# Index scores of a sparse attention step: the order of projection halves, cached products, index chunks and convolution taps on one Trainium2 core

## The chip, the cores and the metric

The kernel runs on one core of one Trainium2 chip. The metric is the device time of one execution in microseconds (us). Three runs of the kernel before took 1020.48, 1022.67 and 1022.98 us; their median, 1022.67 us, is the time before.

## The reference, cut to what matters

One step of a hybrid decoder layer for a prompt group of 1024 tokens and a sample group of 8 tokens over a paged cache of 8192 keys each. One input projection (1024 to 4168 columns) feeds sparse attention and a gated convolution branch. An indexer chooses 256 keys for every query, which are then attended:

```python
def _index_select(qi, wi, ki, q_pos, k_pos, k_sel):
    s = jnp.einsum('thd,ld->thl', qi, ki).astype(jnp.float32) * (IDX_DIM ** -0.5)
    score = jnp.einsum('th,thl->tl', wi.astype(jnp.float32) * (N_IDX_HEADS ** -0.5), jax.nn.relu(s))
    score = jnp.where(k_pos[None, :] <= q_pos[:, None], score, -jnp.inf)
    _, idx = lax.top_k(score, k_sel)
    return idx.astype(jnp.int32)
```

The prompt uses it with its own 1024 index keys, the samples with the cached index keys (`cache_k_idx`). The convolution branch is a causal depthwise convolution of width 31 over 512 channels, with LayerNorm and SiLU behind it. Both branches are gated, go through one output projection and are added to the input. Everything is float32.

## The kernel before, in words

**Stages.** Five instruction streams are written out by hand (TensorE = PE, ScalarE = ACT, VectorE = DVE, GpSimd = POOL, SyncE = SP). They meet only at semaphores, and each engine takes its stream in order. The stages are: normalise and transpose x; project the weight groups in the order kw, glub, glua, qi, v, ga, gc, k, q (line 41 on); index scores; a bitwise search for the 256th largest score; selection, with the k and q projections beside it; attention; output projection. Every PE operation goes through `mm` (L529), so most PE rows carry that line; `plan` hands out the eight PSUM banks, and `begin` waits until the former user of a bank has drained it.

**Convolution taps.** `taps` (L1319, instruction at L1340) runs on DVE. There are 4 channel blocks (c) with 31 taps (j) each, 124 in all, block after block. A tap is one multiply-add over 128x1024 into an accumulator `ctmp`, and waits for the tap before it (`taps_done`). Tap 0 of block c waits for POOL's product of the two gates, `u_done`. Between stretches of taps, DVE does the queries' and weights' operands for the cached scores, the own-key score (`snew_ready`, which PE waits for in `own_score` behind tile 0 of v), and `cached_turn(0)` and `cached_turn(1)`.

**Cached index scores, eight groups n.** POOL gathers pages into `cin` (L1852, four transfers per group, each into a buffer that `cached_turn` of the group before has freed). `cached_turn(n)` (L1306) is four DVE transposes into `ct`, each waiting for its transfer and for PE's product of group n-1 to be through with that buffer. `cached(n)` (L684) on PE multiplies them with the queries and then does the weighted sum of group n-1 (`weigh`); after group 7, that of 7 too. `cached_out(n)` (L1101) and `scores_out` on ACT evacuate them into `sc16a` or `sc16b`, and SP writes each pair to DRAM and reads the whole back as `SD`. `sc16b` lies on the part of `SC` that holds query block 7, so the first index sum of block 7 waits for its last transfer (`scd_out[1]`).

**Prompt index scores, 40 chunks.** `CHUNKS` runs over query blocks i = 2..7, head pairs hp = 0..3 and key columns in steps of 512. Blocks 2 and 3 have one chunk for each head pair (384 and 512 columns), blocks 4 to 7 have two: 512 and a rest of 128, 256, 384 or 512. A chunk holds two units, one for each head e: PE fills two banks at the same time with the two row halves of the array (`index_scores`, L702; two pairs of banks, so chunk n waits for chunk n-2 to be drained); ACT takes each unit through a relu into one of four `relu` buffers (`index_relu`, L1114, instruction L1122), once DVE has used the buffer's last content; DVE weighs it and adds it into `SC` (`weighted`, L1379; L1389 for the first head, L1392 for the others). Each sum waits for the sum just before it (`relu_used`), which is the one it adds to or its neighbour.

**The order of this stage.** Nine slots, the same on PE, ACT and DVE (L715, L1142, L1394). A slot holds one tile of v (8 matmuls of 512 columns; `between` is called in its middle), half of the slot's chunks in the middle of the tile, one cached product, the other half of the chunks, and another cached product. Slots 0 to 4 have no chunks; slots 5, 6 and 7 have 10, 11 and 11; slot 8 the last eight (all of block 7). The cached products stand at the end of slots 1 and 4 (groups 0 and 1), and in slots 5, 6, 7 twice each (2 and 3, 4 and 5, 6 and 7).

**The search.** 32 rounds: DVE (L1420) and ACT (L1159) count how many scores reach a candidate, PE sums the sample's counts over a group of partitions (`group_sum`, L559), and DVE makes the next candidate (L1474). Two more counts (rounds 32 and 33) follow. PE's stream has projection units beside it, `STAGE_UNITS`: the last, 8-row tile of v, 12 pieces of ga and 12 of gc (8 matmuls of 344 columns each), and the first `K_EARLY` = 4 tiles of k (8 matmuls of 512). `pace` (L568) puts one of 34 group sums in front of the matmul at which a multiple of `COLUMNS_PER_SUM` = (all columns)/35 is reached: 86528 columns, 2472 per sum. PE then waits there until the count of that round is in. 

**Behind the search.** The loop over `NORMED` (k tiles 0 to 8, then q) has on PE: tile n if n >= `K_EARLY` (L808), at n = 3 `equal_before` (waits for DVE's `equals_counted`), the transposes of tile n-3, `chosen_before`; on DVE: `norm(n)`, with `chosen` behind tile 0, which waits for `equal_before`.

## Time and profile before

| | |
|---|---|
| median of three runs | 1022.67 us |
| the profiled execution, its own time | 1022.88 us |
| span of the profiled execution | 1021.0 us |
| busy PE, DVE, ACT, POOL | 918.9, 690.4, 348.6, 84.4 us |
| mean granted TensorE clock | 0.947 of 2.4 GHz |

The sums of the prediction are differences of the span (first to last instruction). The profiled execution's own time is 1.9 us more than its span, and 0.2 us above the median. A line of the timeline gives the start and the length of a run of like instructions, and in brackets how long the engine stood idle before it and who ended that. A float32 matmul shows as two records, so "x16" is eight matmuls.

### The profile page before, as it was taken

How to read it: one execution, taken by the hardware profiler on the slowest of the kernel's cores; microseconds unless marked ns; L12 is line 12 of the kernel's file. 1: busy time of each engine (PE TensorE's matmuls, PEld its weight loads, DVE VectorE, ACT ScalarE, POOL GpSimd, SP SyncE). 2: the span in 40 equal slices, each digit the busy share in tenths (PEclk: the TensorE clock that was granted, in tenths of full speed). 3: DMA queues.
4: the chain of work that ended last, by engine and by line, in shares of the span. 5: the costliest groups of instructions: out<-in, count | busy, mean ns of one | idle time of the engine just before them, and what ended most of it. 6: DMA issues, size and time to landing. Idle time of an engine off the chain costs nothing.

```text
span 1021.0 us, 11394 instructions
## 1 busy us (share of the span) xinstructions
PE 918.9 (90%) x3952; PEld 508.5 (50%) x3952; DVE 690.4 (68%) x1532; ACT 348.6 (34%) x750; POOL 84.4 (8%) x89
## 2 busy tenths in 40 slices
PE   3999999999988679999969898797697889999998
PEld 2866666664332236666534244453465555445432
DVE  4218999998587788888898888956587564332101
ACT  6311101101344568888600000313855363321000
POOL 0120112001133000000000000001011010310000
PEclk9899999999999979999989799798799799999999
DMA  8272011213255050020030000005021111321111
GB/s 298 92 206 27 1 47 39 84 47 119 83 167 168 16 177 30 1 83 1 0 103 32 11 31 1 1 1 214 21 64 52 32 35 39 124 83 41 64 63 43
DMA packets 35459, 69.90 MB, mean 68 GB/s; under 512 B 9625, under 2 KB 12097, under 8 KB 35393
## 3 DMA queue, kind: packets, MB, share of 16 engines
q1 hardware_dynamic: 28233, 43.99, 13.3%
q0 software_dynamic: 7168, 25.17, 7.6%
q8 instruction: 32, 0.52, 0.2%
q14 instruction: 26, 0.21, 0.1%
HBM read 58.52 MB, written 11.11 MB: 68 GB/s over the span
## 4 chain that ended last, share of the span: by engine, by line
PE 78%; DVE 13%; ACT 3%; issue 3%; DMA 1%; SPq 1%; DVEq 0%; POOL 0%; ACTq 0%; POOLq 0%
PE ps L529 74%; PE ps L532 5%; DVE SC L1392 2%; DVE ct L1314 1%; DMA xn<-in_x_prompt 1%; DVE pv L1570 1%; ACT PTs L1018 1%; DVE eqm L1420 1%; ACT uT L1191 1%; DVE LB L1571 1%; DVE uT L1776 0%; ACT relu L1122 0%; ACT sqj L1031 0%; DVE junk L1420 0%; DVE zN L1594 0%
## 5 line engine op out<-in xcount | busy, mean ns | idle before, releaser
L529 PE MATMUL ps<-xT,W 128*128 128x344 f32 x960 | 286.9, 457 | 0.0
L529 PEld LDWEIGHTS ps<-xT,W 128*128 128x128 f32 x960 | 180.9, 191 | 90.8 <-issue 3.5
L529 PE MATMUL ps<-W,xT 128*128 128x512 f32 (+3 forms) x576 | 224.8, 546 | 0.0
L1340 DVE SCALAR_TENSOR_TENSOR ctmp<-uT,chw,ctmp 128x1024 f32<-128x1024 f32 x116 | 153.0, 1319 | 4.0
L529 PEld LDWEIGHTS ps<-W,xT 128*128 128x128 f32 (+1 forms) x576 | 95.8, 188 | 114.4 <-issue 113.8
L1159 ACT ACTIVATE sgj<-SC,cand,sense 128x1024 bf16<-128x1024 f32 (+2 forms) x96 | 104.4, 1088 | 25.8 <-DVE cand L1474 20.8
L1018 ACT ACTIVATE PTs<-ps 128x512 f32<-128x512 f32 (+3 forms) x96 | 43.0, 483 | 128.2 <-PE ps L532 123.5
L1807 DVE TENSOR_TENSOR ps<-ps,TP 128x256 f32<-128x256 f32 (+1 forms) x64 | 26.4, 412 | 69.4 <-PE ps L529 69.0
L1204 ACT ACTIVATE nsq<-ps 128x512 f32<-128x512 f32 (+1 forms) x18 | 10.7, 596 | 163.2 <-DVE nss L1583 115.8
L532 PE MATMUL ps<-Cc,Pm 128*128 128x128 f32 x288 | 47.3, 304 | 17.6 <-ACT PTs L1018 17.0
L529 PE MATMUL ps<-W,uT 128*128 128x512 f32 x128 | 60.1, 613 | 0.0
L529 PE MATMUL ps<-W,qT 128*128 128x512 f32 x128 | 58.8, 601 | 0.0
L1812 DVE CUSTOM_DVE_ANT_0 Pm<-ps,SC 128x1024 f32<-128x1024 f32 (+7 forms) x64 | 48.5, 758 | 9.9 <-PE ps L532 7.9
L532 PEld LDWEIGHTS ps<-Cc,Pm 128*128 128x128 f32 x288 | 34.6, 154 | 40.8 <-issue 39.0
L1420 DVE TENSOR_SCALAR_CACHE_REDUCE junk<-SC,cand 128x768 bf16<-128x768 f32 (+2 forms) x67 | 54.6, 815 | 0.0
L1787 DVE TENSOR_TENSOR resid<-resid,ps 128x512 f32<-128x512 f32 (+1 forms) x18 | 12.3, 684 | 60.8 <-PE ps L529 60.8
L1218 ACT ACTIVATE Pm<-Pm,mn 128x1024 f32<-128x1024 f32 (+7 forms) x64 | 49.5, 774 | 9.4 <-DVE mn L1812 8.8
L1885 POOL DMA_INDIRECT KVr<-in_cache_k,idx x16 | 16.0, 1000 | 438.3 <-DVE zq L1598 336.9
L529 PE MATMUL ps<-kiT,qiT 64*128 64x512 f32 (+3 forms) x160 | 37.0, 570 | 15.6 <-ACT relu L1122 15.1
L1392 DVE SCALAR_TENSOR_TENSOR SC<-relu,wI,SC 128x512 f32<-128x512 f32 (+3 forms) x70 | 45.9, 656 | 7.6 <-ACT relu L1122 0.8
L1852 POOL DMA_INDIRECT cin<-in_cache_k_idx,pidx x32 | 34.5, 1079 | 179.6 <-DVE ct L1314 141.9
L1122 ACT ACTIVATE relu<-ps 128x512 f32<-128x512 f32 (+3 forms) x80 | 38.5, 524 | 31.4 <-PE ps L529 16.7
(309 smaller groups left out, 1007.6 us busy)
## 6 DMA issues: line engine op xcount, KB each, us to landing
W<-in_w_in SPq DMA_DIRECT2D x8, 2048.0 KB, 8.9
xn<-in_x_prompt SPq DMA_DIRECT2D x8, 512.0 KB, 7.7
W<-in_w_out SPq DMA_DIRECT2D x1, 4096.0 KB, 13.7
resid<-in_x_prompt SPq DMA_DIRECT2D x16, 256.0 KB
out<-resid SPq DMA_DIRECT2D x16, 256.0 KB
out<-V SPq DMA_DIRECT2D x8, 256.0 KB
out<-zN SPq DMA_DIRECT2D x8, 256.0 KB, 2.0
bias_rows<-tprow SPq DMA_DIRECT2D x1, 1536.0 KB
```

The costliest lines, as they stand in the source:

```text
L529: return nc.tensor.matmul(out, lhsT, rhs, start=start, stop=stop)
L532: return nc.tensor.transpose(out, in_, ident[0:n, 0:n])
L1018: nc.scalar.activation(out, in_, func, scale=scale).then_inc(plan.drain_sem(tag), 1)
L1122: nc.scalar.activation(relu[:, u % 4, 0:width(n)], pt(tag)[:, 0:width(n)], ACT.Relu, scale=HD ** -0.5).then_inc(plan.drain_sem(tag), 1)
L1159: last = nc.scalar.activation(sgj[:, j, 0:s.shape[1]], s, ACT.Sign, bias=cand[:, j:j + 1].bitcast(F32), scale=sense[:, j:j + 1], accum_out ...
L1218: nc.scalar.activation(Pm[:, n % 3, 0:L], Pm[:, n % 3, 0:L], ACT.Exp, bias=mn[:, n % 4:n % 4 + 1], scale=-1.0, accum_out=sums[:, n:n + 1]) ...
L1340: ins = vec.scalar_tensor_tensor(conv[:, c, :] if j == CW - 1 else acc_, src, chw[:, c, j:j + 1], acc_, ALU.mult, ALU.add)
L1392: vec.scalar_tensor_tensor(dst, src, wI[:, i, h:h + 1], dst, ALU.mult, ALU.add).then_inc(relu_used, 1)
L1420: last = vec.tensor_scalar((eqm, junk)[q % 2][:, 0:s.shape[1]], s, against(j), 0.0, op, ALU.add, accum_out=cnt[:, j:j + 1] if j < 6 else c ...
L1807: link(vec.tensor_tensor(s[:, L - bw:L], s[:, L - bw:L], TP[:, h, BAND - bw:BAND], ALU.subtract))
L1812: vec.tensor_tensor_reduce(out=Pm[:, n % 3, 0:L], in0=s, in1=m, scale=1.0, scalar=3.0e38, op0=ALU.add, op1=ALU.min, accum_out=mn[:, n % 4: ...
L1852: pool.indirect_dma_start(out=cin[:, ch % 4, :], out_offset=None, in_=pages_ap, in_offset=bass.IndirectOffsetOnAxis(ap=pidx[:, ch % 8, ch ...
```

## The change

The order of the index stage is written anew. **v runs ahead**: tiles 0 to 4 of v come first, with `cached(0)` behind tile 1 and `cached(1)` behind tile 3 (before: behind tile 4). Then chunks 0 and 1; then six times: half a tile of v (tiles 5, 6, 7), one cached product (groups 2 to 7), six chunks; then chunks 38 and 39. ACT follows in the same order. DVE does `cached_turn` of groups 2 to 7 ahead of chunks 0, 6, 12, 18, 24 and 30, so each stands two chunks earlier in DVE's stream than the product in PE's. **Sums in turns**: for blocks 4 to 7 ACT and DVE take the units of two neighbouring chunks as (n,0), (n+1,0), (n,1), (n+1,1), and a sum waits only for the last one on its own part of `SC`; PE's order stays. **Taps in turns**: block 0 does 19 taps alone; from there taps of two blocks alternate, 105 taps being done when block 3 goes on alone for its last 19. The own-key operands come after 104 taps (before: 96), the wait for its score after 112 (before: 108). **`sc16b` moves** to the area of the dead `gB`/`ctmp`, later `gcT`: the wait of block 7's first sum goes, and ACT waits for the transfers before the first piece of gc. **`K_EARLY` is 2**: tiles 2 and 3 of k leave the search and are computed in the loop behind it, in front of `equal_before`; the columns per group sum are 78336/35 = 2238.

```diff
@@ -213,7 +213,7 @@
     relu = sb("relu", [P, 4, 512], F32, rTP)
-    sc16 = [sb("sc16a", [16, 32, 2, 16], F32, rKV), sb("sc16b", [16, 32, 2, 16], F32, rSC + 12800)]
+    sc16 = [sb("sc16a", [16, 32, 2, 16], F32, rKV), sb("sc16b", [16, 32, 2, 16], F32, rGC)]
     uT = sb("uT", [P, 4, CW - 1 + SEQ], F32, rU)
 ...
@@ -443,25 +443,21 @@
-    FIRST_SLOT, SLOTS = 5, NT + 1
-    CACHED_AT = {1: (0,), 4: (1,), 5: (2, 3), 6: (4, 5), 7: (6, 7)}
-    def chunks_in(s):
-        last = sum(1 for x in CHUNKS if x[0] < NT - 1)
-        if s == SLOTS - 1:
-            return range(last, len(CHUNKS))
-        k, n = s - FIRST_SLOT, SLOTS - 1 - FIRST_SLOT
-        return range(max(k, 0) * last // n, max(k + 1, 0) * last // n)
-    def cached_in(s):
-        return CACHED_AT.get(s, ())
-    def halves(s):
-        c = chunks_in(s)
-        return c[:len(c) // 2], c[len(c) // 2:]
+    V_AHEAD = 5
+    def sums_order():
+        order, n = [], 0
+        while n < len(CHUNKS):
+            two = CHUNKS[n][0] >= 4
+            order += [(n, 0), (n + 1, 0), (n, 1), (n + 1, 1)] if two else [(n, 0), (n, 1)]
+            n += 2 if two else 1
+        return order
+    SUMS = sums_order()
+    TURN_AT = {2 + 6 * j: 2 + j for j in range(6)}
+    TURN_BEFORE = {6 * j: 2 + j for j in range(6)}
 ...
@@ -474,6 +470,19 @@
     NTAP = len(DVE_CHUNKS) * CW
+    ALONE = 19
+    def tap_order():
+        order, at_ = [(0, j) for j in range(ALONE)], [ALONE, 0, 0, 0]
+        for c in range(3):
+            while at_[c] < CW:
+                order += [(c, at_[c]), (c + 1, at_[c + 1])]
+                at_[c] += 1
+                at_[c + 1] += 1
+        return order + [(3, j) for j in range(at_[3], CW)]
+    TAPS = tap_order()
 ...
@@ -488,7 +497,7 @@
-    K_EARLY = 4
+    K_EARLY = 2
     STAGE_UNITS = DURING_SEARCH[EVACUATED_EARLY:] + [("k", t) for t in range(K_EARLY)]
 ...
@@ -712,25 +721,28 @@
-        for s in range(SLOTS):
-            one, two = halves(s)
-            def between():
-                for n in one:
-                    index_scores(n)
-            if s < NT:
-                natural("v", s, 2, between)
-            else:
-                between()
-            if s == 0:
+        for t in range(V_AHEAD):
+            natural("v", t, 2)
+            if t == 0:
                 own_score()
-            for n in cached_in(s)[:1]:
-                cached(n)
-            for n in two:
+            if t == 1:
+                cached(0)
+            if t == V_AHEAD - 2:
+                cached(1)
+        def turn_chunks(j):
+            cached(2 + j)
+            for n in range(2 + 6 * j, min(8 + 6 * j, len(CHUNKS))):
                 index_scores(n)
-            for n in cached_in(s)[1:]:
-                cached(n)
+        for n in range(2):
+            index_scores(n)
+        for j in range(0, 6, 2):
+            natural("v", V_AHEAD + j // 2, 2, lambda: turn_chunks(j))
+            turn_chunks(j + 1)
+        for n in range(38, len(CHUNKS)):
+            index_scores(n)
         for g, m in STAGE_UNITS:
 ...
@@ -1111,11 +1123,11 @@
-        def index_relu(n):
-            for e in range(2):
+        def index_relu(lo, hi):
+            for u in range(lo, hi):
+                n, e = SUMS[u]
                 tag = ("ix", n, e)
-                u = 2 * n + e
                 act.wait_ge(*plan.full(tag))
 ...
@@ -1136,21 +1148,25 @@
                 a, n = piece_rows(m)
+                if m == 0:
+                    act.wait_ge(scd_out[1], 128)
                 piece_out(g, m, gcT[:, m // 3, a:a + n], sT[:, 3], ACT.Silu)
-        for s in range(SLOTS):
-            one, two = halves(s)
-            for n in one:
-                index_relu(n)
-            if s < NT:
-                evacuate("v", s)
-            for n in cached_in(s)[:1]:
-                cached_out(n)
-            for n in two:
-                index_relu(n)
-            for n in cached_in(s)[1:]:
-                cached_out(n)
+        for t in range(V_AHEAD):
+            evacuate("v", t)
+            if t == 1:
+                cached_out(0)
+            if t == V_AHEAD - 2:
+                cached_out(1)
+        for n in range(len(CHUNKS)):
+            if n % 2:
+                index_relu(2 * n - 2, 2 * n + 2)
+            t = V_AHEAD + (n - 7) // 12
+            if n % 12 == 7 and t < NT:
+                evacuate("v", t)
+            if n + 1 in TURN_AT:
+                cached_out(TURN_AT[n + 1])
         ev = EVACUATED_EARLY
 ...
@@ -1318,19 +1334,21 @@
             for m in range(lo, hi):
-                c, j = DVE_CHUNKS[m // CW], m % CW
+                c, j = TAPS[m]
                 if m == 0:
 ...
                     v.wait_ge(u_done, 3 * c + 3)
+                    if c >= 2:
+                        v.wait_ge(taps_done, TAPS.index((c - 2, CW - 1)) + 1)
                 src = uT[:, c, j:j + SEQ]
-                acc_ = ctmp[:, m // CW % 2, :]
+                acc_ = ctmp[:, c % 2, :]
                 if j == 0:
 ...
                 else:
-                    v.wait_ge(taps_done, m)
+                    v.wait_ge(taps_done, TAPS.index((c, j - 1)) + 1)
                     if j == CW - 1:
 ...
@@ -1345,7 +1363,7 @@
         vec.tensor_tensor(sT[:, 1], sT[:, 1], sT[:, 0], ALU.mult).then_inc(made["decode_u"], 1)
-        taps(2 * CW + 5, NTAP - 28)
+        taps(2 * CW + 5, NTAP - 20)
         v.wait_ge(*plan.full("Qb"))
 ...
@@ -1369,39 +1387,35 @@
         vec.reduce_sum(sn[:, 8:9], sn[:, 0:8], AXX).then_inc(snew_ready, 1)
-        taps(NTAP - 28, NTAP - 16)
+        taps(NTAP - 20, NTAP - 12)
         v.wait_ge(*plan.full("sn"))
         vec.tensor_tensor(SD[:, SEG:SEG + 1], pt("sn")[:, 0:1], const("negcol"), ALU.add).then_inc(plan.drain_sem("sn"), 1)
-        taps(NTAP - 16, NTAP - 8)
+        taps(NTAP - 12, NTAP - 8)
         cached_turn(1)
 ...
-        def weighted(n):
+        def weighted(u):
+            n, e = SUMS[u]
             i, hp, a = CHUNKS[n]
-            if (i, hp, a) == (NT - 1, 0, 0):
-                v.wait_ge(scd_out[1], 128)
-            for e in range(2):
-                u, h = 2 * n + e, 2 * hp + e
-                src, dst = relu[:, u % 4, 0:width(n)], sc(i)[:, a:a + width(n)]
-                v.wait_ge(*plan.drained(("ix", n, e)))
-                if h == 0:
-                    vec.tensor_scalar(dst, src, wI[:, i, 0:1], None, ALU.mult).then_inc(relu_used, 1)
-                else:
-                    v.wait_ge(relu_used, u)
-                    vec.scalar_tensor_tensor(dst, src, wI[:, i, h:h + 1], dst, ALU.mult, ALU.add).then_inc(relu_used, 1)
-        for s in range(FIRST_SLOT, SLOTS):
-            one, two = halves(s)
-            for n in cached_in(s)[:1]:
-                cached_turn(n)
-            for n in one:
-                weighted(n)
-            for n in cached_in(s)[1:]:
-                cached_turn(n)
-            for n in two:
-                weighted(n)
+            h = 2 * hp + e
+            src, dst = relu[:, u % 4, 0:width(n)], sc(i)[:, a:a + width(n)]
+            v.wait_ge(*plan.drained(("ix", n, e)))
+            if h == 0:
+                vec.tensor_scalar(dst, src, wI[:, i, 0:1], None, ALU.mult).then_inc(relu_used, 1)
+                return
+            for w in range(u):
+                if CHUNKS[SUMS[w][0]][0::2] == (i, a):
+                    last = w
+            v.wait_ge(relu_used, last + 1)
+            vec.scalar_tensor_tensor(dst, src, wI[:, i, h:h + 1], dst, ALU.mult, ALU.add).then_inc(relu_used, 1)
+        for n in range(len(CHUNKS)):
+            if n in TURN_BEFORE:
+                cached_turn(TURN_BEFORE[n])
+            if n % 2 == 0:
+                for u in range(2 * n, 2 * n + 4):
+                    weighted(u)
 ...
```

## Rows read from the trace of the kernel before

**Rows 1.** The page, part 4: the chain that ended last, shares by engine.

```profile
PE 78%; DVE 13%; ACT 3%; issue 3%; DMA 1%; SPq 1%; DVEq 0%; POOL 0%; ACTq 0%; POOLq 0%
```

**Rows 2.** Busy time by stretch: us, busy PE, PEld, DVE, ACT, POOL, granted clock, DMA.

```profile
350.00:363.70 13.70, 5.68 (x16) 1.73 (x16) 11.53 (x18) 7.05 (x12) 0.29 (x1) 0.75 0.06 20
...
372.00:504.00 132.00, 132.00 (x479) 85.44 (x478) 111.24 (x390) 111.20 (x215) 0.00 (x0) 1.00 0.11 37
```

**Rows 3.** Who waited for whom from 264 to 364: us in total, times, longest.

```profile
PE ps L529 <- ACT relu L1122: 15.1, 14, 3.5
DVE ct L1314 <- PE ps L529: 13.7, 4, 6.1
```

**Rows 4.** Timeline of DVE before the index sums: start, length, instruction, idle before it.

```profile
212.42 15.79 DVE L1340 SCALAR_TENSOR_TENSOR ctmp<-uT,chw,ctmp 128x1024 f32<-128x1024 f32 x12
232.05 0.16 DVE L1374 TENSOR_TENSOR SD<-ps,Cc 128x1 f32<-128x1 f32 x1 [3.84 <-PE ps L529]
...
256.30 1.28 DVE L1340 SCALAR_TENSOR_TENSOR uT<-uT,chw,ctmp 128x1024 f32<-128x1024 f32 x1
263.69 4.62 DVE L1314 STREAM_TRANSPOSE ct<-cin 128x1024 f32<-128x1024 f32 x4 [6.10 <-PE ps L529]
```

**Rows 5.** The same of DVE at the start: multiply-adds without waits between them.

```profile
18.02 3.68 DVE L1291 SCALAR_TENSOR_TENSOR xn<-xn,rst,gB 128x1024 f32<-128x1024 f32 x3
```

**Rows 6.** Timeline from `cached(1)` over half a tile of v to the first index sum.

```profile
261.68 1.95 PE L529 MATMUL ps<-ct,Qb 128*32 128x512 f32 x16
...
264.37 3.70 PE L529 MATMUL ps<-W,xT 128*128 128x512 f32 x8
...
268.00 1.56 PE L529 MATMUL ps<-kiT,qiT 64*128 64x384 f32 x8
...
269.47 0.42 DVE L1389 TENSOR_SCALAR SC<-relu,wI 128x384 f32<-128x384 f32 x1 [1.16 <-ACT relu L1122]
```

**Rows 7.** Timeline of chunks 10, 11 (block 4), PE's next chunk; relus of block 7.

```profile
292.29 1.35 PE L529 MATMUL ps<-kiT,qiT 64*128 64x512 f32 x8
...
293.45 1.42 ACT L1122 ACTIVATE relu<-ps 128x512 f32<-128x512 f32 x4 [3.46 <-PE ps L529]
...
294.68 1.35 PE L529 MATMUL ps<-kiT,qiT 64*128 64x512 f32 x8 [1.04 <-ACT relu L1122]
...
345.38 2.06 ACT L1122 ACTIVATE relu<-ps 128x512 f32<-128x512 f32 x4 [0.47 <-PE ps L529]
...
350.63 0.60 ACT L1122 ACTIVATE relu<-ps 128x512 f32<-128x512 f32 x1 [3.18 <-DVE SC L1389]
```

**Rows 8.** Timeline: weighted sums 6 and 7, block 7's sums, PE's first group sum.

```profile
341.45 1.02 PE L529 MATMUL ps<-drelu,Wb 128*16 128x512 f32 x2
...
344.22 1.99 PE L529 MATMUL ps<-kiT,qiT 64*128 64x512 f32 x8
...
350.05 0.49 DVE L1389 TENSOR_SCALAR SC<-relu,wI 128x512 f32<-128x512 f32 x1 [5.61 <-DMA decode_scores<-sc16b]
...
351.89 11.01 DVE L1392 SCALAR_TENSOR_TENSOR SC<-relu,wI,SC 128x512 f32<-128x512 f32 x13
...
364.75 0.56 PE L529 MATMUL ps<-c,group 128*128 128x1 f32 x2 [6.72 <-DVE eqm L1420]
```

**Rows 9.** Timeline of DVE late in the search: the candidates of two rounds.

```profile
496.54 0.17 DVE L1474 SCALAR_TENSOR_TENSOR cand<-tk,candx 128x7 uint32<-128x7 uint32 x1
...
500.46 0.17 DVE L1474 SCALAR_TENSOR_TENSOR cand<-tk,candx 128x7 uint32<-128x7 uint32 x1
```

**Rows 10.** Timeline of PE behind the last round: group sums 31 and 33, `equal_before`.

```profile
503.94 0.28 PE L529 MATMUL ps<-c,group 128*128 128x1 f32 x2
...
515.97 0.38 PE L529 MATMUL ps<-c,group 128*128 128x1 f32 x2 [2.83 <-DVE eqm L1420]
...
525.72 0.28 PE L529 MATMUL ps<-dC,Cc 128*128 128x1 f32 x2
```

**Rows 11.** Timeline of DVE there: `chosen`.

```profile
528.49 0.15 DVE L1511 TENSOR_TENSOR dsc<-cnt,ps 128x1 f32<-128x1 f32 x1
```

## The prediction

> **What bounds the kernel now.** I read the chain of the page first: three quarters of the span are PE [rows 1]. That is an average, so the next view is busy time by stretch [rows 2]. In the search (372 to 504) PE is busy for all of its 132 us, at the full granted clock. At the end of the index stage (350 to 363.7) it is busy for 5.7 of 13.7 us, DVE for 11.5, and the granted clock is 0.75. The waits of that stage say why [rows 3]: PE waits 15.1 us for ACT's relus, in 14 pieces, and DVE 13.7 us in `cached_turn` for PE's product of the group before. DVE also waits 5.6 us once for the transfer that frees the place of `sc16b` [rows 8]. Neither engine bounds this stage alone; they wait for each other. The search cannot start before the last index sum, which ends at 362.9 (351.89 + 11.01); PE's first group sum is at 364.75 [rows 8]. A measurement of this kernel can tell about 0.3%, 3.1 us, from no change.
>
> **Part 1: taps in turns.** One tap takes 1.28 us, and a tap that waits for the one before it starts every (15.79 - 1.28) / 11 = 1.32 us [rows 4]. The nearest instruction of this form and size without such a wait is the normalisation of x: (3.68 - 1.28) / 2 = 1.20 us [rows 5]. That gives 0.12 us for each of some 86 taps, 10 us, less about 2 us at the first tap of block 1, which now waits for POOL. None of it is on the path. DVE is done with the own key at 212.4 and idles 3.84 us up to 232.05, where PE's `own_score` behind tile 0 of v answers [rows 4]. Without any gain the eight taps moved ahead of the own key (10.5 us) would have it ready at 223, still before PE asks. Behind the answer stand 4 taps (5.3 us), a turn of transposes (4.6) that cannot start before `cached(0)` near 239.5, and 8 taps (10.5): DVE is done near 254.8. Gain and cost on the path: nothing; the cover is PE's tiles of v.
>
> **Part 2: v ahead.** Half a tile of v is 3.63 us with the switch behind it (268.00 - 264.37), a tile 6.9; a product and the weighted sum behind it are 2.69 (264.37 - 261.68) [rows 6]. `cached(1)` and tile 4 change places: the product stands at 261.68 - 6.9 = 254.8. DVE's turn of group 2, which waited until 263.69 [rows 4], can go at 255.3, and its 4.6 us lie beside tile 4. Chunk 0 no longer stands behind half a tile: it starts at 268.00 - 3.63 = 264.4, and its first sum 1.47 us later (269.47 - 268.00) [rows 6], at 265.9.
>
> **Part 3: the slots.** In PE's stream each of six slots holds half a tile 3.6, product and weighted sum 2.7, and a switch 0.1: 6.4 us, and six chunks. What do these take? PE needs 0.86 us for 512 columns (3.43 us for four matmuls), but it has only two pairs of banks. From a chunk's start to its first relu 1.16 us pass, and from there to PE's next start 1.23 (294.68 - 293.45), which is 0.49 for one relu and 0.74 for the second and the way back [rows 7]; relus of 512 follow each other every (2.06 - 0.60) / 3 = 0.49 us. So a pair of chunks took 2.39 us. Now a relu of chunk n+1 is put between the two of chunk n, and chunk n is drained later: 1.16 + 0.49 + 0.20 (a relu of 128) + 0.74 = 2.6 us in block 4, 2.7 in block 5. In blocks 6 and 7 the relu in between also waits until PE has filled chunk n+1 (0.64 and 0.86 us): 1.16 + 0.64 + 0.41 + 0.74 = 2.95 and 1.16 + 0.86 + 0.49 + 0.74 = 3.25 us. DVE needs less. A sum of 512 takes 0.75 us and starts every (11.01 - 0.75) / 12 = 0.855 behind a wait [rows 8]; with the overlap of rows 5 (0.08 us) every 0.67, so 2.7 us for the four units of a pair in block 7 and 1.9 in block 4. **PE's loop through ACT is the limit, and the turns make it longer.** I take these values, since each term is a row; the ends are the old 2.39 us a pair, and DVE at its old pace.
>
> The Trainium skill, "VectorE: DVE Perf Modes", section "The DRAIN you can't avoid", says that the next Vector instruction cannot issue until the pipe is empty, and that leaving out semaphores in between gained nothing. By that rule both kinds of turns give nothing; the trace does not agree, with 1.20 against 1.32 us [rows 4, 5], though on another instruction.
>
> **The sum.** Chunks 0 and 1 take 1.3 us from 264.4; 6.4 behind them chunk 2 is at 272.1 and its first sum at 273.6. Here DVE is the limit: 8 sums of blocks 2 and 3 without turns 6.1 us, the transposes of group 3 4.6, the rest of the product, the weighted sum and a switch 1.6: chunk 8 at 285.9. From here PE: chunks 8 to 13 are 2 x 2.6 + 1.2 (last pair, PE alone) + 6.4 = 12.8, to 298.7; 14 to 19 are 2.6 + 2.7 + 1.5 + 6.4 = 13.2, to 311.9; 20 to 25 are 2 x 2.7 + 1.7 + 6.4 = 13.5, to 325.4; 26 to 31 are 2 x 2.95 + 1.7 + 6.4 = 14.0. Group 7 has a second weighted sum: 2.77 us (344.22 - 341.45) [rows 8] in place of 0.95, so chunk 32 is at 341.2. Four pairs of 3.25 are 13.0, the last relu and sum 1.2: the last sum ends at 355.4, against 362.9. **Gain 7.5 us.** DVE, with 4.6 + 5.7 to 8.1 us a slot, keeps up.
>
> Three small edits. The wait for `sc16b` is gone; since DVE then works at PE's pace, its 5.6 us are not a gain of their own but part of the 7.5. `SD` is read when those transfers are in, 5.8 us behind the chunk that follows the weighted sums (350.05 - 344.22), so from 347; even if the read takes as long again, it is in at 353 and not late. ACT's new wait in front of gc's first piece is for the same transfers, over long before; behind it are only ACT's counts, and it costs nothing. POOL's last mask and SP's order stay, and so do the 1.85 us from the last sum to PE's first group sum.
>
> **Part 4: two tiles of k.** In the search PE is never idle, so it paces the rounds: (503.94 - 364.75) / 31 = 4.49 us each [rows 8, 10]. A round that PE does not hold up takes 3.92 us (500.46 - 496.54) [rows 9]. The sum of round 31 stood behind 76800 columns and would stand behind 69456: 13 matmuls of 0.87 and two of 0.59 less, 12.5 us. Rounds of 4.09 us are still above 3.92, so PE keeps pacing. Behind it DVE's two last counts are no faster: the sum of round 33 comes 12.0 us behind that of round 31 (515.97 - 503.94) [rows 10], and PE will idle nearly 4 us there, not 2.8. Then PE does 24 matmuls where it did 9 (9.75 us, with a lower clock behind the wait): 15 x 0.87 = 13.0 us more. `equal_before` comes 12.0 + 9.75 + 13.0 = 34.8 us behind round 31's sum, on the old scale at 491.4 + 34.8 = 526.2, against 525.72. DVE came to `chosen` only at 528.49 [rows 11]; now it stands waiting for some 10 us and goes at 526.5. **Gain 2.0 us.** Moving the tiles shortens the search by 12.5 us and gives 10.5 back, because PE has no less to do. The work behind `chosen` is the same and moves as a whole.
>
> The total is 9.5 us. The profiled execution took 1022.88 us, 1.9 more than its span: 1013.4; as that run is 0.2 above the median, **1013.2 us**.
>
> **Rivals.**
> - *The pair does not get longer.* ACT's relus are earlier than I think and the turns do help DVE. Pairs of 2.39 on PE's path spare 2.8 us up to chunk 32, and block 7 at DVE's 2.7 another 2.2: last sum at 350.4 (if `SD` is not late), 14.5 us in all, 1008.2 us. For it: DVE's units are short; against: PE's wait for relus is the longest [rows 3].
> - *The clock falls in block 7.* PE would be busy 1.7 of 3.25 us there. In 350 to 363.7 it was busy 5.7 of 13.7 us, at 0.75, between its levels of 1.2 and 2.4 GHz [rows 2]. At 1.2 GHz both chunks of a pair cost 0.86 us more, part of it behind relus: some 1.3 us a pair, 5 in all, 1018.4 us.
> - *Turns gain nothing on DVE.* At the pace behind a wait, the pairs of blocks 4 to 7 cost DVE 2.6, 2.9, 3.15 and 3.4 us, 48 in all; with four turns (18.5) and 5 of stalls behind products from 287.9 on it ends at 359.4: 1017.2 us. It is also what the cited rule gives.
> - *Slower: the tiles of k lose their cover.* If a round has a floor near 4.5 us (ACT's pieces of the gates now lie closer together), the search does not shorten, `equal_before` is 34.8 us behind 503.94, and `chosen` goes 10.5 us later; less 7.5, that is 3.0 slower, 1025.7 us. It decides from a mean round of 4.39: 0.3 over my 4.09, times 31, eats the 9.5 us. Against it: the undisturbed 3.92.
>
> **How the numbers follow.** Forecast 0.48 (its own range 1010 to 1016.5), pairs not longer 0.15, clock 0.15, no gain on DVE 0.12, k uncovered 0.10. The range leaves out the last and the far ends of the others: 1007 to 1020.5. Faster by over 0.3% (below 1019.6) are the first four but for the slow ends of the third and fourth: 0.83; within 0.3% 0.08; slower 0.09.
>
> **What would show it.** First sum near 266, last near 355; pairs of 2.6 to 3.25 us with PE's waits for relus in between; no wait of the transposes of groups 3 to 7 for PE; granted clock 1.00 up to 340. Mean round 4.09, first group sum to round 31's 127 us and not 139; PE idle 4 us ahead of the sum of round 33; DVE idle about 10 us ahead of `chosen`. I am wrong if pairs take 2.4, if rounds stay near 4.5, or if the work behind `chosen` changes in length by over 2 us.

## The result, and the profile after

| | before | after |
|---|---|---|
| median | 1021.36 us (5 runs, 1020.48 to 1022.98) | 1009.74 us (5 runs, 1003.82 to 1014.94) |
| profiled execution, its span | 1022.88, 1021.0 us | 1009.64, 1007.8 us |
| chunk 0 to first group sum | 96.75 us | 93.10 us |
| first group sum to `chosen` | 163.74 us | 162.16 us |
| `chosen` to the end | 492.5 us | 487.9 us |

The new kernel's time is 0.988 of that before (95% interval 0.984 to 0.992): the median is 11.6 us lower, 1009.7 us where 1013.2 was forecast. The new kernel's runs are spread over 11 us, so below I compare marks within one profiled execution of each kernel; a median alone does not settle 3 us. The marks are the starts of PE's first matmul of chunk 0, of PE's first group sum, and of DVE's `chosen`.

The page of the kernel after: busy times, and the chain that ended last.

```profile
PE 912.7 (91%) x3952; PEld 507.6 (50%) x3952; DVE 677.9 (67%) x1532; ACT 346.0 (34%) x750; POOL 103.4 (10%) x89
...
PE 79%; DVE 12%; ACT 4%; issue 3%; DMA 1%; SPq 1%; DVEq 0%; ACTq 0%; POOL 0%; POOLq 0%
```

Busy time by stretch in the kernel after (columns as in [rows 2]).

```profile
264.00:350.00 86.00, 72.10 (x312) 28.07 (x310) 63.39 (x93) 42.70 (x96) 21.06 (x23) 1.00 0.38 118
350.00:360.50 10.50, 4.72 (x15) 1.50 (x15) 9.13 (x23) 7.10 (x13) 0.29 (x1) 0.89 0.30 82
```

Who waited for whom from 264 to 360 (us in total, times, longest), PE and then DVE.

```profile
PE ps L538 <- ACT relu L1134: 13.8, 13, 1.3
...
DVE SC L1411 <- ACT relu L1134: 14.0, 10, 5.2
DVE SC L1405 <- ACT relu L1134: 10.0, 5, 4.6
```

Against [rows 3] DVE's 13.7 us in `cached_turn` are gone, and the transfer of `sc16b` is in no wait. PE's wait for the relus is hardly shorter, but its longest piece fell from 3.5 to 1.3 us: they are now the steady gap of each pair. DVE waits for ACT instead, so the loop of PE and ACT sets the pace, as forecast.

The timeline of PE in the index stage: chunk 0; chunks 8 to 13; chunks 32 to 37; the first group sum.

```profile
264.69 1.56 PE L538 MATMUL ps<-kiT,qiT 64*128 64x384 f32 x8
...
286.15 1.35 PE L538 MATMUL ps<-kiT,qiT 64*128 64x512 f32 x8
288.82 1.35 PE L538 MATMUL ps<-kiT,qiT 64*128 64x512 f32 x8 [1.32 <-ACT relu L1134]
291.35 1.35 PE L538 MATMUL ps<-kiT,qiT 64*128 64x512 f32 x8 [1.18 <-ACT relu L1134]
...
341.57 1.99 PE L538 MATMUL ps<-kiT,qiT 64*128 64x512 f32 x8
344.81 1.99 PE L538 MATMUL ps<-kiT,qiT 64*128 64x512 f32 x8 [1.26 <-ACT relu L1134]
348.03 1.99 PE L538 MATMUL ps<-kiT,qiT 64*128 64x512 f32 x8 [1.23 <-ACT relu L1134]
...
357.79 0.35 PE L538 MATMUL ps<-c,group 128*128 128x1 f32 x2 [4.55 <-DVE eqm L1434]
```

One line is a pair of chunks: 2.67 and 2.53 us from start to start in block 4, 3.24 and 3.22 in block 7. The first group sum is 6.96 us earlier than before (364.75 in [rows 8]): 3.31 because chunk 0 is earlier, 3.65 because the stage behind it is shorter.

DVE in the same stage: taps in turns, taps of block 3 alone, the own key, the turn of group 2, and the last sums.

```profile
137.60 22.80 DVE L1358 SCALAR_TENSOR_TENSOR ctmp<-uT,chw,ctmp 128x1024 f32<-128x1024 f32 x19
...
213.53 10.51 DVE L1358 SCALAR_TENSOR_TENSOR ctmp<-uT,chw,ctmp 128x1024 f32<-128x1024 f32 x8
232.18 0.16 DVE L1392 TENSOR_TENSOR SD<-ps,Cc 128x1 f32<-128x1 f32 x1 [8.13 <-PE ps L538]
...
256.95 4.62 DVE L1330 STREAM_TRANSPOSE ct<-cin 128x1024 f32<-128x1024 f32 x4 [0.77 <-PE ps L538]
...
353.01 2.93 DVE L1411 SCALAR_TENSOR_TENSOR SC<-relu,wI,SC 128x512 f32<-128x512 f32 x4 [0.28 <-ACT relu L1134]
```

A tap in turns starts every (22.80 - 1.28) / 18 = 1.20 us, one that waits for the tap just before it every (10.51 - 1.28) / 7 = 1.32. What the turns gain, DVE spends idle at the own key: 8.13 us, where it was 3.84 [rows 4].

PE behind the last round: group sums 32 and 33 and `equal_before`, and then DVE's `chosen`.

```profile
487.85 0.38 PE L538 MATMUL ps<-c,group 128*128 128x1 f32 x2
...
495.90 0.56 PE L538 MATMUL ps<-c,group 128*128 128x1 f32 x2 [3.27 <-issue]
496.32 23.48 PE L538 MATMUL ps<-W,xT 128*128 128x512 f32 x48
519.63 0.28 PE L538 MATMUL ps<-dC,Cc 128*128 128x1 f32 x2
...
519.95 0.15 DVE L1525 TENSOR_TENSOR dsc<-cnt,ps 128x1 f32<-128x1 f32 x1 [11.48 <-PE ps L538]
```

The first row is the sum of round 32, the second that of round 33, the last one; that of round 31 is at 483.60. The profile names no releaser for PE's 3.27 us; what PE waits for at that place in its stream is the count of round 33. PE does 24 matmuls (48 records) between the last sum and `equal_before`, and DVE stands 11.48 us in front of `chosen`, where it did not wait at all before [rows 10, 11].

### The profile page after: what moved, and what is told of

The parts are those of the page before. It is cut to its first block, busy times and chain, and to the rows that moved or that the text cites. A ratio compares the mean times of both kernels' runs of the same rounds, so it can differ in the third digit from the quotient of the medians.

```text
span 1007.8 us, 11396 instructions
## 1 busy us (share of the span) xinstructions
PE 912.7 (91%) x3952; PEld 507.6 (50%) x3952; DVE 677.9 (67%) x1532; ACT 346.0 (34%) x750; POOL 103.4 (10%) x89
## 4 chain that ended last, share of the span: by engine, by line
PE 79%; DVE 12%; ACT 4%; issue 3%; DMA 1%; SPq 1%; DVEq 0%; ACTq 0%; POOL 0%; POOLq 0%
PE ps L538 75%; PE ps L541 4%; ACT relu L1134 1%; DVE pv L1584 1%; DMA xn<-in_x_prompt 1%; ACT PTs L1030 1%; DVE SC L1411 1%; ACT uT L1207 1%; DVE LB L1585 1%; DVE zN L1608 0%; DVE uT L1790 0%; ACT sqj L1043 0%; DVE ps L1821 0%; DVE pv L1550 0%; DVE mcum L1510 0%
## 5 line engine op out<-in xcount | busy, mean ns | idle before, releaser
L538 PE MATMUL ps<-W,xT 128*128 128x512 f32 (+3 forms) x576 | 221.4, 540 | 0.0
L1358 DVE SCALAR_TENSOR_TENSOR ctmp<-uT,chw,ctmp 128x1024 f32<-128x1024 f32 x116 | 144.9, 1298 | 1.3
L1234 ACT ACTIVATE Pm<-Pm,mn 128x1024 f32<-128x1024 f32 (+7 forms) x64 | 49.5, 774 | 10.9 <-DVE mn L1826 10.3
L1411 DVE SCALAR_TENSOR_TENSOR SC<-relu,wI,SC 128x512 f32<-128x512 f32 (+1 forms) x70 | 42.7, 653 | 15.6 <-ACT relu L1134 14.0
L538 PE MATMUL ps<-kT,qT 64*128 64x512 f32 (+3 forms) x192 | 43.7, 563 | 6.1 <-DVE mn L1826 3.6
L538 PE MATMUL ps<-kiT,qiT 64*128 64x512 f32 (+3 forms) x160 | 33.9, 539 | 13.8 <-ACT relu L1134 13.8
## 6 DMA issues: line engine op xcount, KB each, us to landing
W<-in_w_out SPq DMA_DIRECT2D x1, 4096.0 KB, 13.7
```

Of the source, the lines that this page charges most:

```text
L538: return nc.tensor.matmul(out, lhsT, rhs, start=start, stop=stop)
L1234: nc.scalar.activation(Pm[:, n % 3, 0:L], Pm[:, n % 3, 0:L], ACT.Exp, bias=mn[:, n % 4:n % 4 + 1], scale=-1.0, accum_out=sums[:, n:n + 1]) ...
L1358: ins = vec.scalar_tensor_tensor(conv[:, c, :] if j == CW - 1 else acc_, src, chw[:, c, j:j + 1], acc_, ALU.mult, ALU.add)
L1411: vec.scalar_tensor_tensor(dst, src, wI[:, i, h:h + 1], dst, ALU.mult, ALU.add).then_inc(relu_used, 1)
```

## The experiments

All are the changed kernel with one edit, except e2, which is the kernel before with one. The marks, in us:

| kernel | median | ratio to before (95% interval) | chunk 0 to first group sum | from there to `chosen` | `chosen` to the end |
|---|---|---|---|---|---|
| e1_four_k_in_search | 1014.25 | 0.990 (0.986-0.994) | 93.09 | 162.54 | 484.8 |
| e2_only_two_k | 1020.35 | 0.998 (0.996-1.000) | 99.94 | 159.46 | 490.5 |
| e3_sums_in_chunk_order | 1012.45 | 0.989 (0.986-0.993) | 92.72 | 162.48 | 491.4 |
| e4_taps_block_by_block | 1009.95 | 0.989 (0.986-0.992) | 93.17 | 159.32 | 490.6 |
| e5_relus_in_chunk_order | 1011.94 | 0.990 (0.987-0.992) | 90.27 | 163.51 | 492.6 |
| e6_sc16b_on_block_7 | 1017.92 | 0.996 (0.994-0.998) | 96.51 | 163.74 | 492.7 |
| e7_later_sum_earlier_equal | 996.68 | 0.977 (0.974-0.979) | 93.08 | 151.89 | 484.4 |
| e8_both | 994.42 | 0.974 (0.971-0.976) | 90.26 | 151.76 | 491.0 |
| e9_later_sum_alone | 1004.90 | 0.989 (0.983-0.994) | 93.10 | 155.86 | 488.3 |
| e10_equal_earlier_alone | 1001.25 | 0.986 (0.980-0.991) | 93.19 | 152.43 | 488.4 |
| e11_e7_with_four_k | 1012.87 | 0.993 (0.990-0.996) | 93.08 | 163.92 | 492.8 |

One execution of e8 took 3778.93 us and is left out of its ratio and median (with it the median is 996.28); nothing shows what held it. The ratio is estimated from all executions of the two kernels, those of the kernel before taken in the same session (medians 1020.56 to 1022.05), and is not always the quotient of two medians (for e10 that is 0.981). Against the changed kernel's 0.984 to 0.992 only the intervals of e2, e6, e7 and e8 stand apart, and that of e11 does from e7's; between the others and the changed kernel the medians settle nothing.

How far do the marks repeat? The seven executions with the changed kernel's index stage (changed, e1, e4, e7, e9, e10, e11) have 93.08 to 93.19 us from chunk 0 to the first group sum. The order before has only two, 96.75 and, in e2, 99.94, though e2 changes nothing there. In e2 three of PE's six cached products in the stage took 3.2 to 3.3 us, in the kernel before one took 3.6; all others took 1.94. The granted clock of the stage was 0.90 in e2 and 0.94 in the kernel before. So the new order's stage is 3.6 to 6.8 us shorter, and its gain is known no better than that.

### The tiles of k: e1 and e2

```diff
-    K_EARLY = 2
+    K_EARLY = 4
```

> The changed kernel with four tiles of k in the search again. Theory (the tiles only change places): the first group sum stays at 357.8; the sum of round 31 moves from 483.6 back by 12.5 us to about 496.5; PE's wait ahead of the sum of round 33 falls from 3.3 to some 2.8 us; DVE does not wait in front of chosen and reaches it near 521.5, 1.5 to 2 us later than in the changed kernel; the whole is 1.5 to 2 us slower if nothing else hangs on it. Rival (the move also keeps PE's clock up behind chosen): the first tile of k behind chosen takes 9.8 us again and not 7.0, and the whole is 4 to 6 us slower than the changed kernel, 7 to 9 us faster than the kernel before.

e2 makes the reverse edit (4 to 2) in the kernel before.

> The kernel before with K_EARLY = 2 and nothing else changed. Theory (the tiles only change places): first group sum at 364.8, mean round 4.09, sum of round 31 near 491.3, chosen near 526.9 with DVE waiting 11 us in front of it: 1.5 to 2 us faster than the kernel before. Rival (clock): another 3 to 5 us are gained behind chosen, 5 to 7 us in all. Third possibility (cover lost): rounds stay near 4.5 us and the time is longer than before by 2 us or more.

e1's PE at the last sum and `equal_before`, and its `chosen`; this profiled execution is shifted by some 15 us from its start on (see the last section).

```profile
372.68 0.56 PE L538 MATMUL ps<-c,group 128*128 128x1 f32 x2 [4.55 <-DVE eqm L1434]
...
510.66 0.28 PE L538 MATMUL ps<-c,group 128*128 128x1 f32 x2
...
522.69 0.59 PE L538 MATMUL ps<-c,group 128*128 128x1 f32 x2 [2.84 <-DVE eqm L1434]
...
532.40 0.28 PE L538 MATMUL ps<-dC,Cc 128*128 128x1 f32 x2
...
535.22 0.15 DVE L1525 TENSOR_TENSOR dsc<-cnt,ps 128x1 f32<-128x1 f32 x1
```

With four tiles (e1) the sum of round 31 comes 138.0 us behind the first, with two (the changed kernel) 125.8: two tiles make the rounds 12.2 us shorter. Yet `chosen` comes 162.2 us behind the first group sum, against 162.5: all but 0.4 us is given back as DVE's wait, where 1.5 to 2 was expected. The rival of e1 is not settled: its median is 4.5 us above the changed kernel's, as that rival says, and the first tile of k behind `chosen` took PE 9.31 us against 7.11. But the whole part behind `chosen` is 3.1 us shorter in e1's profiled execution (484.8 for 487.9), and its six executions lie between 1006.92 and 1021.82 us.

In the kernel before (e2) the edit brings `chosen` 4.3 us nearer to the first group sum (159.46 for 163.74) and leaves a wait of 8.65 us in front of it.

```profile
528.11 0.15 DVE L1511 TENSOR_TENSOR dsc<-cnt,ps 128x1 f32<-128x1 f32 x1 [8.65 <-PE ps L529]
```

Its median is 1.7 us below that of before (1020.35 for 1022.05), which the interval does not tell from nothing; counted from chunk 0, `chosen` is only 1.1 us nearer, since the index stage was longer in that execution. At `chosen` the one kernel gains 0.4 us by the two tiles and the other 4.3. Of these 3.9 us, 2.8 lie between the last sum and `equal_before` (the last section, on PE's clock); the rest is that the rounds up to 31 came closer together by 13.2 us there and 12.2 here.

### Turns of sums and relus: e3 and e5

e3 takes the turns away on ACT and DVE alike:

```diff
-            two = CHUNKS[n][0] >= 4
+            two = False
```

> The changed kernel with ACT's relus and DVE's sums of blocks 4 to 7 in the order of the chunks (a sum still waits only for the last on its own part of SC). Theory (PE's loop through ACT is the limit and the turns lengthen it): pairs of chunks in PE's stream take 2.4 us while DVE can follow, not 2.5 to 3.2; chunk 32 starts 2 to 3 us earlier than 341.6; in block 7 DVE becomes the limit at about 3.0 us a pair; last sum near 352 to 353 against 355.9, so 2 to 4 us faster. Rival (DVE is the limit and the turns helped): last sum later than 355.9, by up to 4 us, and DVE without waits for relus.

e5 leaves them on DVE and takes them from ACT:

```diff
-                n, e = SUMS[u]
+                n, e = u // 2, u % 2
...
-                    act.wait_ge(relu_used, u - 3)
+                    act.wait_ge(relu_used, SUMS.index(((u - 4) // 2, u % 2)) + 1)
...
-            src, dst = relu[:, u % 4, 0:width(n)], sc(i)[:, a:a + width(n)]
+            src, dst = relu[:, (2 * n + e) % 4, 0:width(n)], sc(i)[:, a:a + width(n)]
```

> The changed kernel with ACT's relus in the order of the chunks, while DVE keeps its turns (each relu buffer is given back by DVE's place in its own order). Theory (the turns of the relus lengthen PE's loop, the turns of the sums shorten DVE's; the chunk-order run had lost on DVE what it won on PE): pairs of chunks 2.4 us in blocks 4 to 6, 2.7 in block 7 (DVE at 0.67 us a unit); chunk 32 near 339, last sum near 351.3, first group sum near 353.2, 4.6 us earlier than in the changed kernel. Rival (independent sums do not start every 0.67 us): block 7's pairs stay at 3.0 to 3.2 us and the last sum is later than 353.

Block 7 in e3: two pairs of PE, and DVE's sums.

```profile
344.76 2.11 PE L538 MATMUL ps<-kiT,qiT 64*128 64x512 f32 x8 [0.40 <-ACT relu L1134]
347.12 2.11 PE L538 MATMUL ps<-kiT,qiT 64*128 64x512 f32 x8 [0.25 <-ACT relu L1134]
...
346.00 9.85 DVE L1411 SCALAR_TENSOR_TENSOR SC<-relu,wI,SC 128x512 f32<-128x512 f32 x13
```

The same in e5, with PE's first group sum.

```profile
342.19 2.11 PE L538 MATMUL ps<-kiT,qiT 64*128 64x512 f32 x8 [0.40 <-ACT relu L1134]
344.55 2.11 PE L538 MATMUL ps<-kiT,qiT 64*128 64x512 f32 x8 [0.25 <-ACT relu L1134]
...
342.97 9.36 DVE L1411 SCALAR_TENSOR_TENSOR SC<-relu,wI,SC 128x512 f32<-128x512 f32 x14
...
354.17 0.56 PE L538 MATMUL ps<-c,group 128*128 128x1 f32 x2 [4.86 <-DVE eqm L1434]
```

With relus in the order of the chunks PE's pair is 2.36 us again, where turns make it 3.22. In e3 DVE then becomes the limit: a sum starts every (9.85 - 0.75) / 12 = 0.76 us on average. The gaps alternate (starts at 346.00, 346.67, 347.52): 0.85 us where the unit adds to the sum just before it, 0.67 where it starts on another part of `SC`. In e5 a sum starts every (9.36 - 0.75) / 13 = 0.66 us, and the first group sum comes 2.8 us sooner behind chunk 0 than in the changed kernel (90.27 for 93.10); 4.6 was expected. e3 was expected to be 2 to 4 us faster and is 0.4 in this stage. So turns on ACT cost 2.8 us (e5 against the changed kernel) and turns on DVE gain 2.5 (e5 against e3, 92.72), and the change pairs the one with the other. In the median of e5 the 2.8 us do not appear: `chosen` comes 1.4 us later behind the first sum, and the part behind it is 4.8 us longer, both with less granted clock (0.96 for 0.97, and 0.92 for 0.93).

### Taps and sc16b: e4 and e6

```diff
-    TAPS = tap_order()
+    TAPS = [(c, j) for c in range(4) for j in range(CW)]
```

> The changed kernel with the taps block after block (the points at which DVE does other work stay at 104, 112, 116 taps). Theory (tiles of v cover the taps): DVE's wait for the own key's score near 232.2 falls from 8.1 to below 1 us or to nothing, DVE finishes the taps within 1 us of 256.2, the transposes of group 2 start at most 1.5 us later, chunk 0 starts at 264.7 as before, and the last sum is within 0.5 us of 355.9: no difference in time. Rival (the taps were part of the gain): chunk 0 or the last sum moves later by 3 us or more.

DVE's own-key row in e4:

```profile
221.89 10.51 DVE L1358 SCALAR_TENSOR_TENSOR ctmp<-uT,chw,ctmp 128x1024 f32<-128x1024 f32 x8
232.37 0.16 DVE L1392 TENSOR_TENSOR SD<-ps,Cc 128x1 f32<-128x1 f32 x1
```

The wait of 8.13 us is gone, and the stage did not move: 93.17 us, for 93.10. The turns of taps only made DVE's wait longer; without them DVE arrives just as PE answers. (POOL did change; see the last section.)

```diff
-    sc16 = [sb("sc16a", [16, 32, 2, 16], F32, rKV), sb("sc16b", [16, 32, 2, 16], F32, rGC)]
+    sc16 = [sb("sc16a", [16, 32, 2, 16], F32, rKV), sb("sc16b", [16, 32, 2, 16], F32, rSC + 12800)]
...
-                if m == 0:
-                    act.wait_ge(scd_out[1], 128)
...
+            if (i, h, a) == (NT - 1, 0, 0):
+                v.wait_ge(scd_out[1], 128)
```

> The changed kernel with sc16b back on the place of block 7 and the wait of block 7's first sum back. Theory: the sum waits until the transfers are in, near 347.1 in place of 343.4 (3.7 us), then DVE catches up at 0.67 us a unit because PE and ACT have filled the buffers; last sum 1.5 to 2.5 us later than 355.9. Rival (the wait was worth its whole 5.6 us, or the whole of its 3.7): last sum 3.7 us later or more. Other rival (the transfers come no earlier than the rest anyway): no difference.

The first sum of block 7 in e6, and two of PE's pairs behind it.

```profile
347.09 0.88 DVE L1405 TENSOR_SCALAR SC<-relu,wI 128x512 f32<-128x512 f32 x2 [7.90 <-DMA decode_scores<-sc16b]
...
344.48 1.99 PE L538 MATMUL ps<-kiT,qiT 64*128 64x512 f32 x8 [1.26 <-ACT relu L1134]
349.46 3.65 PE L538 MATMUL ps<-kiT,qiT 64*128 64x512 f32 x8 [3.00 <-ACT relu L1134]
```

The four relu buffers fill, ACT stops, and PE stands 3.00 us: the stage is 3.4 us longer (96.51), where 1.5 to 2.5 was expected. The span of its profiled execution is 9.5 us longer than the changed kernel's: 3.4 are this wait, 1.6 lie between the first sum and `chosen` and 4.8 behind it, where the work is the same (less 0.4 ahead of chunk 0). The median of twelve executions is 8.2 us above the changed kernel's, and the intervals lie apart, so more than the 3.4 us recurs from one execution to the next. Why it does is not shown.

### Away with the wait in front of chosen: e7 and its parts

e7 makes the last group sum due 2048 columns later and calls `equal_before` one tile earlier in the loop, so that 12 matmuls stand between them where there were 24. e9 has the first edit alone, e10 the second, e8 both together with those of e5, e11 both with `K_EARLY = 4`.

```diff
-            while summed[0] < GROUP_SUMS and summed[0] * COLUMNS_PER_SUM <= emitted[0]:
+            while summed[0] < GROUP_SUMS and summed[0] * COLUMNS_PER_SUM + 2048 * (summed[0] == GROUP_SUMS - 1) <= emitted[0]:
...
-            if n == 3:
+            if n == 2:
                 equal_before()
```

> The changed kernel with two places of PE's stream moved: the group sum of round 33 stands four matmuls later (in the middle of tile 1 of k), and equal_before stands behind tile 2 of k, tile 3 behind it. Theory (in the changed kernel the two tiles stand in front of DVE's chosen, which waits 8.6 to 11.5 us): PE's wait ahead of the sum of round 33 goes (3.3 us), chosen no longer waits and stands about 150.6 us behind the first group sum, the rest of PE's wait for chosen (2.6 us) is filled by tile 3, and the second product with the strict matrix comes 156 us behind the first group sum and not 162 to 165. 6 to 9 us faster than the changed kernel. Rival (DVE bounds the stage behind chosen, so that nothing depends on when PE comes): the same or up to 2 us faster.

> The changed kernel with both edits: relus in the order of the chunks with DVE's turns kept, and the two moved places behind the search. Theory: the gains add, 4.6 and 6 to 9 us, 10 to 13 us under the changed kernel, near 998 us. Rival: one hides behind the other and only the larger remains.

> The changed kernel with one of the two edits of e7_later_sum_earlier_equal: the last group sum is due 2048 columns later, equal_before stays where it was. Theory (PE's own queue sets chosen, because with two k tiles fewer in the rounds 48 products still stand between the last sum and the equal offsets): the wait of 3.27 us before the last sum goes, 40 products are left behind it, the equal offsets come about 3.3 us earlier (516.3 on the scale of the changed kernel), chosen at about 158.9 us behind the first group sum instead of 162.2, DVE still idle for about 8 us before it, and the time falls by 3 to 4 us to about 1006. Rival (the whole 13 us of e7 come from the wait that went and from the clock that it pulled down): 998.

> The changed kernel with the other edit of e7_later_sum_earlier_equal alone: equal_before one natural tile earlier, so that 32 products instead of 48 stand between the last sum and it. Theory: the wait of 3.27 us before the last sum stays, the equal offsets come 7 to 8 us earlier (about 512), chosen at about 154.5 us behind the first group sum, DVE idle for about 4 us before it; the time falls by 7 to 8 us to about 1002. Rival (one edit is as good as both, since DVE can't be there before 508): 997.

> e7_later_sum_earlier_equal with four k tiles beside the rounds again. Theory (e7 gains because DVE, early by the shorter rounds, no longer waits for PE; with four k tiles DVE itself is late and there is no wait to save): the sum of round 31 comes 12 us later than with two k tiles, chosen at 162 to 163 us behind the first group sum, DVE without a wait before it, time 1009 to 1014, as in e1_four_k_in_search (1014.25) less at most the 2.84 us that PE waited for the last sum. Rival (e7 gains by moving PE work behind chosen, whatever the rounds do): chosen at about 152 us behind the first group sum and 997 us.

(Where these texts say 48, 40 or 32 products, they count records; two are one matmul.) e7's last sum, its matmuls, `equal_before`, and `chosen`:

```profile
496.21 0.34 PE L538 MATMUL ps<-c,group 128*128 128x1 f32 x2
496.41 10.55 PE L538 MATMUL ps<-W,xT 128*128 128x512 f32 x24
506.80 0.28 PE L538 MATMUL ps<-dC,Cc 128*128 128x1 f32 x2
...
508.70 0.15 DVE L1525 TENSOR_TENSOR dsc<-cnt,ps 128x1 f32<-128x1 f32 x1
```

PE's wait of 3.27 us and DVE's of 11.48 are both gone; `chosen` is 10.3 us nearer to the first group sum (151.89 for 162.16), and the median 13.1 us below that of the changed kernel (6 to 9 was expected), 25.0 us below that of the kernel before in the same session (1021.68). e9, e10 and e11 at `chosen`:

```profile
512.98 0.16 DVE L1525 TENSOR_TENSOR dsc<-cnt,ps 128x1 f32<-128x1 f32 x1 [5.20 <-PE ps L538]
```

```profile
510.95 0.16 DVE L1525 TENSOR_TENSOR dsc<-cnt,ps 128x1 f32<-128x1 f32 x1 [1.78 <-PE ps L538]
```

```profile
520.46 0.15 DVE L1525 TENSOR_TENSOR dsc<-cnt,ps 128x1 f32<-128x1 f32 x1
```

Each edit takes part of DVE's wait (5.20 and 1.78 us left). e9 brings `chosen` 6.3 us nearer, not the 3.3 of PE's wait alone: its 20 matmuls between the last sum and `equal_before` took 0.87 us each, the changed kernel's 24 took 0.99. With four tiles of k in the search there was no wait to take: `chosen` stays 163.9 us behind the first sum, with e7's placement as without (162.5 in e1). So e7's gain is the 12 us that the shorter rounds had made and the change had left standing in front of `chosen`. e8 has the shortest way to `chosen` of all (242.0 us from chunk 0; e7 245.0, the changed kernel 255.3): up to there the gains of e5 and e7 add. But its part behind `chosen` is 6.6 us longer than e7's in the profiled execution, and the ratios of the two overlap; it is not shown to be faster than e7.

## Why the prediction was right

- **Part 1** (taps, nothing on the path): 1.20 us a tap in turns against 1.32 was forecast and measured, and e4 shows that it buys nothing. The cover, PE's tiles of v, held. The own key was ready at 213.5 us, and at 221.9 in e4, where I had put 223 without any gain.
- **The Trainium skill's rule** ("VectorE: DVE Perf Modes", "The DRAIN you can't avoid"), which I had read as saying that turns give nothing on DVE: the runs do not agree with that reading, on the taps (1.20 for 1.32) and on the sums (0.66 in e5, 0.855 before). The same section says "A next op that is not held starts earlier", and I had left that out. The rival built on it is out by PE's rows too: no product waits for DVE's transposes, and the last sum ended at 355.9, not 359.4.
- **Part 2**: chunk 0 forecast at 264.4, measured 264.69; `cached(1)` forecast at 254.8, measured 254.9. The turn behind it, forecast at 255.3, waited for PE and began at 256.95; tile 4 of v covered that too.
- **Part 3**: pairs of 2.6 us in block 4 and 3.25 in block 7 forecast, 2.53 to 2.67 and 3.22 to 3.24 measured; chunk 8 at 285.9, measured 286.15; chunk 32 at 341.2, measured 341.57; last sum at 355.4, measured 355.94 (353.01 + 2.93). The gain was to be 7.5 us and is 7.0 against the one execution that the forecast was made from; e2 shows that the order before can take 3.2 us more, so this close a match is in part luck. One sentence was too general: that the turns lengthen the pair is right (e3, e5), but it is ACT's turns alone, and DVE's are worth having; I did not see that the two can be had apart. That of `sc16b`'s wait, "part of the 7.5", is shown by e6: 3.4 us.
- **The clock rival** for block 7 is out: 1.00 up to 350 and 0.89 behind it, with pairs no longer than forecast. *The pair does not get longer* is out by the rows of PE.
- **Part 4**: sum of round 31 forecast 126.7 us behind the first, measured 125.8; PE's wait for the last sum nearly 4, measured 3.27; from there to `equal_before` 22.75, measured 23.7; DVE's wait about 10, measured 11.48. The gain was to be 2.0 us, and is 1.6. "Moving the tiles shortens the search by 12.5 us and gives 10.5 back" is borne out by e1: 12.2 us and 11.8. The rival with uncovered tiles is out: rounds of 125.8 / 31 = 4.06 us.
- **The step that failed** is the last of Part 4: "the work behind `chosen` is the same and moves as a whole". It is the same in instructions (2036 matmul records in both), but took 487.9 us, not 492.5. By my own sign of being wrong, a change of over 2 us there, this step failed. Its 4.7 us stand beside 8.5 from the steps before `chosen`, where I had 9.5; together they are the 13.2 by which the profiled spans differ. I had put the term at nothing, and the total came as near as it did because the term is small and the other steps fell 1.0 short. 3.0 of the 4.7 us lie between `chosen` and the end of PE's first tile of k behind it:

```profile
531.98 9.93 PE L529 MATMUL ps<-W,xT 128*128 128x512 f32 x16
```

```profile
523.24 7.11 PE L538 MATMUL ps<-W,xT 128*128 128x512 f32 x16
```

The first line is of the kernel before, the second of the changed one. The two tiles of k alone do not decide this: with two in the search the same eight matmuls took 7.11 us in e2, e4 and e9 too, but 8.81 in e3 and 10.0 in e5 and e6.

What stays open is how much of the 11.6 us of the medians comes from behind `chosen`: the marks are of one execution each, and that part varies by itself (below).

## What to carry to other kernels

Work moved out of a stage that PE paces has to be put down somewhere, and if that is in front of the next product that another engine waits for, the stage's gain turns into that engine's wait; look for the due point of that product and move it with the work (e7: `chosen` 10.3 us nearer and the median 13.1 us lower, from two lines). Where two engines take units in the same new order, test the order on each alone: here it helps the one with a chain of dependent sums and harms the one that gives the banks back. Work done faster in front of a wait that stays is no gain (the taps). And read a mark from more than one execution: here the same work behind `chosen` took 8 us more in one than in another.

## What the runs showed of the hardware that I had not expected

The same instructions take different times from one profiled execution to the next, by the granted clock. PE's busy time behind `chosen` in the kernel before and in the changed kernel (columns as in [rows 2]):

```profile
528.49:1021.00 492.51, 438.15 (x2036) 224.96 (x2036) 280.05 (x731) 130.71 (x292) 32.05 (x32) 0.92 0.16 53
```

```profile
519.95:1007.80 487.85, 434.21 (x2036) 222.55 (x2034) 280.08 (x730) 130.63 (x292) 32.06 (x32) 0.93 0.15 50
```

PE is busy 3.9 us less with the same matmuls; DVE, ACT and POOL are level. Ten of the thirteen profiled executions have these 2036 records behind `chosen` (in e7, e8 and e10 part of the k tiles moved there as well). In them this part took 484.8 to 492.8 us, PE being busy for 432.5 to 438.8. Four of the ten lie within 0.4 us of each other (before, e5, e6, e11: 492.5 to 492.8), though they are four different kernels. What decides it was not tried; that e6's median is high as well leaves open that an edit far ahead can draw it.

A wait of PE is not always followed by a slower stretch. The ten us behind the same wait of 3.3 us in front of the last sum, in the changed kernel and then in e10:

```profile
496.00:506.00 10.00, 10.00 (x19) 4.51 (x20) 8.90 (x24) 0.60 (x1) 0.00 (x0) 0.72 0.09 23
```

```profile
496.00:506.00 10.00, 9.40 (x24) 4.41 (x25) 9.00 (x23) 1.19 (x2) 0.00 (x0) 1.00 0.07 18
```

The granted clock was 0.72 in the one, a mixture of 2.4 and 1.2 GHz, and 1.00 in the other. From the last sum to `equal_before` the same 24 matmuls took 23.7 us in the changed kernel and 20.9 in e4 and e2, and this is why e2 gains 4.3 us at `chosen` over the kernel before where the change gains 1.6. Even the start of the kernel does it: in e1's profiled execution the first projection ran at a granted clock of 0.56 from 30 to 60 us, in the changed kernel at 0.99, and everything behind it came some 15 us later.

```profile
30.00:60.00 30.00, 30.00 (x167) 29.39 (x166) 0.97 (x12) 5.73 (x27) 4.12 (x4) 0.56 0.21 71
```

```profile
30.00:60.00 30.00, 29.65 (x209) 24.59 (x208) 5.32 (x12) 8.86 (x34) 8.09 (x8) 0.99 0.58 197
```

Taps in turns hold POOL up. One of its products of the gates beside the taps, in the changed kernel and then in e4, which differs in the order of DVE's taps alone:

```profile
152.09 12.68 POOL L1882 TENSOR_TENSOR uT<-uT,glua_r 128x344 f32<-128x344 f32 x1 [15.25 <-ACT glua_r L1030]
```

```profile
152.30 2.00 POOL L1882 TENSOR_TENSOR uT<-uT,glua_r 128x344 f32<-128x344 f32 x1 [17.03 <-ACT glua_r L1030]
```

The one instruction lasted 12.68 us beside taps that start every 1.20 us, and 2.00 beside taps that start every 1.32; it ended at 164.77, when DVE's unbroken run of taps had ended at 163.99. Another, at 124.22, lasted 10.15 us where it takes 0.79 in e4. POOL is busy 103.4 us in all for 86.3 in e4. It cost no time in this kernel (e4's stage is as long), but DVE's first tap of block 1 waited 1.43 us for POOL, and where POOL's work is urgent it would matter.
